# Cached keys and values loaded in 512 KB blocks, three at a time, and B's attention in another order of work

## The reference

```python
def diff_attn_sample(q, k_new, v_new, k_past, v_past, lam):
    s = concatenate([einsum('bqhcd,bkhcd->bhcqk', q, k_past), einsum('bqhcd,bkhcd->bhcqk', q, k_new)], -1) * scale
    p = softmax(s)
    pd = p[:, :, 0] - lam * p[:, :, 1]
    return einsum('bhqk,bkhe->bqhe', pd[..., :p_len], v_past) + einsum(..., pd[..., p_len:], v_new)

def fox_sample(q, k_new, v_new, logf_new, k_past, v_past, logf_past):
    f_cum = cumsum(concatenate([logf_past, logf_new], 1), 1)
    s_past = einsum('bqhd,bkhd->bhqk', q, k_past) * scale + f_q[..., None] - f_past
    s_new = einsum('bqhd,bkhd->bhqk', q, k_new) * scale + f_q[..., None] - f_new     # causal
    p = softmax(concatenate([s_past, s_new], -1))
    return einsum('bhqk,bkhd->bqhd', p[..., :p_len], v_past) + einsum(..., p[..., p_len:], v_new)
```

## Time and profile before

| | us |
|---|---|
| median of 3 runs | 2518.02 (2517.57 to 2519.05) |
| the profiled execution | 2516.69 |
| its span, first to last instruction | 2514.2 |
| PE busy | 2463.0 |
| VectorE busy | 1687.4 |
| ScalarE busy | 1134.2 |

### The profile page before, as it was taken

How to read it: one execution, slowest core, us unless ns; L and a number is a source line. 1 busy time by engine, 2 the same in 40 slices (tenths; PEclk the granted TensorE clock), 3 DMA queues, 4 the chain that set the end, 5 groups by cost and what they waited for, 6 DMA issues and landing times.

```text
span 2514.2 us, 46820 instructions
## 1 busy us (share of the span) xinstructions
PE 2463.0 (98%) x18869; PEld 2333.4 (93%) x18869; DVE 1687.4 (67%) x2936; ACT 1134.2 (45%) x2261; POOL 192.3 (8%) x136
## 2 busy tenths in 40 slices
PE   8999999999898999999999999999998899999998
PEld 8999999888678999999988999999986599999998
DVE  7777676322797886758625786858626677868585
ACT  6443444101785543435413553525327755535254
POOL 0000000543000000000044000000120000000000
PEclk9999999999999999999999999999999999999999
DMA  4323232233762232323233332222359631322222
GB/s 129 91 72 95 70 99 61 82 117 102 293 236 76 63 105 62 99 76 91 62 80 125 106 109 81 74 87 72 114 192 314 226 109 47 111 79 74 86 72 80
DMA packets 267136, 271.45 MB, mean 108 GB/s; under 512 B 13785, under 2 KB 224034, under 8 KB 266930
## 3 DMA queue, kind: packets, MB, share of 16 engines
q1 hardware_dynamic: 261184, 253.45, 32.4%
q10 hardware_dynamic: 5746, 15.12, 1.7%
HBM read 255.02 MB, written 13.51 MB: 107 GB/s over the span
## 4 chain that ended last, share of the span: by engine, by line
PE 90%; DVE 5%; ACT 2%; issue 2%; DMA 1%; DVEq 0%; POOL 0%; ACTq 0%
PE PS L769 40%; PE PS L875 24%; PE PS L956 10%; PE PS L719 7%; PE PS L707 2%; PE PS L1014 1%; PE PS L702 1%; PE PS L1157 1%; PE PS L1115 1%; DMA R<-in_cache_b_k_dram 1%; PE PS L1076 1%; PE PS L1087 1%; DVE x_area L2050 0%; DVE R L2005 0%; ACT R L1646 0%
## 5 line engine op out<-in xcount | busy, mean ns | idle before, releaser
L769 PE MATMUL PS<-x_area,w_area 128*128 128x320 f32 x3096 | 482.1, 309 | 0.0
L769 PEld LDWEIGHTS PS<-x_area,w_area 128*128 128x128 f32 x3096 | 461.0, 188 | 0.2 <-DVE w_area L1991 0.2
L875 PE MATMUL PS<-r_area,w_area 128*128 128x320 f32 x2568 | 393.3, 309 | 0.0
L875 PEld LDWEIGHTS PS<-r_area,w_area 128*128 128x128 f32 x2568 | 380.7, 188 | 0.8 <-DVE r_area L2183 0.8
L1435 ACT ACTIVATE w_area<-R 128x512 fp32r<-128x512 f32 x341 | 212.7, 628 | 200.4 <-PE PS L769 133.0
L1982 DVE TENSOR_TENSOR w_area<-R,w_area 128x768 fp32r<-128x768 f32 (+2 forms) x143 | 132.4, 926 | 218.5 <-ACT w_area L1420 216.9
L1991 DVE TENSOR_TENSOR w_area<-R,w_area 128x512 fp32r<-128x512 f32 x341 | 234.4, 688 | 47.6 <-ACT w_area L1435 41.8
L1420 ACT ACTIVATE w_area<-R 128x768 fp32r<-128x768 f32 (+2 forms) x143 | 117.0, 818 | 308.2 <-PE PS L875 281.2
L875 PE MATMUL PS<-v_area,w_area 128*128 128x320 f32 x1620 | 253.5, 309 | 0.0
L956 PE MATMUL PS<-w_area,xn_hi 128*128 128x512 f32 x800 | 251.0, 395 | 0.0
L875 PEld LDWEIGHTS PS<-v_area,w_area 128*128 128x128 f32 x1620 | 241.5, 188 | 0.3 <-DVE v_area L2183 0.3
(11 more groups left out here) (297 smaller groups left out, 3566.6 us busy)
## 6 DMA issues: line engine op xcount, KB each, us to landing
R<-in_w_ffn_up_dram SPq DMA_DIRECT2D x88, 512.0 KB, 3.9
R<-in_w_ffn_gate_dram SPq DMA_DIRECT2D x84, 512.0 KB, 3.9
R<-in_w_ffn_down_dram SPq DMA_DIRECT2D x96, 384.0 KB, 3.2
vreg<-in_cache_a_v_dram SPq DMA_DIRECT2D x8, 2048.0 KB, 9.0
vreg<-in_cache_b_v_dram SPq DMA_DIRECT2D x8, 2048.0 KB, 9.5
R<-in_cache_a_k_dram SPq DMA_DIRECT2D x14, 1024.0 KB, 7.2
R<-in_cache_b_k_dram SPq DMA_DIRECT2D x14, 1024.0 KB, 9.8
R<-in_w_qkv_a_dram SPq DMA_DIRECT2D x24, 512.0 KB, 3.8
```

Source lines behind the costliest of these rows:

```text
L769: last = pe.matmul(PS[:, bank, 0:HT], a[:, k, :], b[:, k, :], start=(start and k == 0 and a is hi and b is x_hi), stop=(k == 3 and a is lo ...
L875: last = pe.matmul(out[:, h, :], a[slot][:, w], x[:, h * HT:(h + 1) * HT], start=(k == 0 and a is w_hi and x is hi), stop=(k == n - 1 and ...
```

## The change

1. Keys are loaded in four blocks of 128 rows x all 1024 columns (512 KB, rows of 4 KB) instead of two halves of 4 heads. `Knat[:, k, :]` is row block `k`. Blocks 0 and 2 share one semaphore, 1 and 3 the other; SP waits for the landing of block `k - 2` before it asks for block `k`.
2. Values are loaded in four blocks in the same manner.
3. `key_pair(b, j)` becomes `key_turn(b, j)`: it turns row block `j` of all 8 heads (again 16 half turns) and needs that block alone. Its reads go to `kTc[:, :, j * 128 ...]`.
4. SP asks for each key block as soon as it is turned, and splits the values around the last key block. At the start of A it waits for the last projection tile, then asks for all of values 0, then keys 1, then the first tile of the output weights; before, keys 1 were first.
5. B's order of steps changes on PE, ScalarE and VectorE. A's order stays, but for the new key step.

```diff
-        Knat = R1[:, 0:4096].rearrange("p (s k c) -> p s k c", s=2, k=PB)
+        Knat = R1[:, 0:4096].rearrange("p (k c) -> p k c", k=PB)
...
+        def keys_landed(b, k):
+            return 16 + (b - 1) * 32 + (k // 2 + 1) * 16
+        def values_landed(x, b, k):
+            return ("AB".index(x) * DB + b) * 32 + (k // 2 + 1) * 16
...
+                def keys(b, k):
+                    at = sem(f"k_in{x}{k % 2}")
+                    sp.wait_ge(at, keys_landed(b, k) - 16)
+                    sp.dma_start(Knat[:, k, :], key_rows[x][b, k * P:(k + 1) * P, :]).then_inc(at, 16)
+                def values(b, blocks):
+                    for k in blocks:
+                        at = sem(f"v_in{k % 2}")
+                        if k >= 2:
+                            sp.wait_ge(at, values_landed(x, b, k) - 16)
+                        sp.dma_start(Vc[:, k, :], vc[b][k * P:(k + 1) * P, :]).then_inc(at, 16)
...
-                sp.wait_ge(sem("kt_ready" + x), 4)
-                keys(1, 0)
                 if x == "A":
+                    sp.wait_ge(w_used, BASE["oa"])
+                    values(0, range(PB))
+                    sp.wait_ge(sem("kt_readyA"), 8)
+                    for k in range(PB):
+                        keys(1, k)
                     tile(BASE["oa"], SLOT["oa"], *cols(w_o_a[0], SLOT["oa"], 0))
-                    sp.wait_ge(sem("kt_readyA"), 8)
-                    keys(1, 1)
-                    sp.wait_ge(w_used, BASE["oa"])
-                else:
+                else:
+                    sp.wait_ge(sem("kt_readyB"), 8)
+                    keys(1, 0)
+                    keys(1, 1)
                     sp.wait_ge(w_used, BASE["ob"] - 1)
                     rows(0)
                     forget(0, 0)
+                    keys(1, 2)
+                    keys(1, 3)
...
-                    if i + 2 < DB:
-                        sp.wait_ge(sem("kt_ready" + x), (i + 1) * 8 + 4)
-                        keys(i + 2, 0)
-                    if f_scr is not None and i + 2 < PAIR:
-                        sp.wait_ge(sem("nb_ready" + x), i * 4 + 4)
-                        rows(i + 2)
+                    for k in range(3):
+                        if more:
+                            sp.wait_ge(sem("kt_ready" + x), (i + 1) * 8 + 2 * k + 2)
+                            keys(i + 2, k)
+                        if k == 1 and f_scr is not None and i + 2 < PAIR:
+                            sp.wait_ge(sem("nb_ready" + x), i * 4 + 4)
+                            rows(i + 2)
                     sp.wait_ge(sem("pv_ready" + x), i * 2 + 2)
-                    values(i + 1)
-                    if i + 2 < DB:
+                    values(i + 1, (0, 1))
+                    if more:
                         sp.wait_ge(sem("kt_ready" + x), (i + 1) * 8 + 8)
-                        keys(i + 2, 1)
+                        keys(i + 2, 3)
+                    values(i + 1, (2, 3))
...
 # PE, key step
-                    for h in range(2):
-                        at = (2 * j + h) % 4 * P
-                        for k in range(PB):
-                            for r in range(2):
-                                to = (4 * h + k) * 64
-                                last = half_flip(PS[:, 3 + 4 * r, to:to + 64], Knat[:, j // 2, k, at:at + P], r)
+                    for h in range(PAIR):
+                        for r in range(2):
+                            last = half_flip(PS[:, 3 + 4 * r, 64 * h:64 * h + 64], Knat[:, j, h * P:(h + 1) * P], r)
...
 # PE, a round of B
                         stream_scores(i)
+                        stream_flips(i - 1)
                         output_columns(i - 1)
-                        stream_flips(i - 1)
+                        key_turn(i + 1, 0)
                         prompt_scores(x, i, (3,))
                         turn(i, 0)
-                        key_pair(i + 1, 0)
                         stream_turn(i)
                         turn(i, 1)
-                        key_pair(i + 1, 1)
+                        key_turn(i + 1, 1)
+                        prompt_scores(x, i + 1, (0, 1))
+                        stream_turn_new(i)
                         turn(i, 2)
-                        stream_turn_new(i)
-                        key_pair(i + 1, 2)
-                        prompt_scores(x, i + 1, (0, 1))
+                        key_turn(i + 1, 2)
                         stream_values(i)
-                        key_pair(i + 1, 3)
+                        key_turn(i + 1, 3)
+                        turn(i, 3)
                         prompt_scores(x, i + 1, (2,))
-                        turn(i, 3)
...
 # ScalarE, a round of B
                         stream_exps(i)
+                        key_turn(i + 1, 0)
                         turned(i, 0)
-                        key_pair(i + 1, 0)
                         differences(i)
+                        key_turn(i + 1, 1)
                         turned(i, 1)
-                        key_pair(i + 1, 1)
+                        exps(i, 3)
+                        key_turn(i + 1, 2)
                         turned(i, 2)
-                        exps(i, 3)
-                        key_pair(i + 1, 2)
                         exps(i + 1, 0)
+                        key_turn(i + 1, 3)
                         exps(i + 1, 1)
-                        key_pair(i + 1, 3)
...
 # VectorE, a round of B
                         stream_peaks(i)
+                        stream_output(i - 1)
                         output_columns(i - 1)
-                        stream_output(i - 1)
                         combine(i, 1)
+                        peaks(i, (3,))
+                        stream_norms(i)
+                        differences(i)
                         combine(i, 2)
-                        peaks(i, (3,))
-                        differences(i)
-                        stream_norms(i)
                         new_differences(i)
```

More of the change, by code:

```diff
@@ L586, in load_attention @@
                     rows(1)
-                    sp.wait_ge(sem("kt_readyB"), 8)
-                    keys(1, 1)
                     sp.wait_ge(w_used, BASE["ob"])
-                values(0)
+                    values(0, range(PB))
                 for i in range(DB - 1):
+                    more = i + 2 < DB
                     if f_scr is not None:
@@ L994, in first_keys @@
             def first_keys(x, h, bank):
-                pe.wait_ge(sem(f"k_in{x}{h // 4}"), 16)
+                for s in range(2):
+                    pe.wait_ge(sem(f"k_in{x}{s}"), 16)
                 if h >= 2:
@@ L999, in first_keys @@
                 for k in range(PB):
-                    last = flip(PS[:, bank, k * P:(k + 1) * P], Knat[:, h // 4, k, (h % 4) * P:(h % 4 + 1) * P])
+                    last = flip(PS[:, bank, k * P:(k + 1) * P], Knat[:, k, h * P:(h + 1) * P])
                 last.then_inc(sem("kt_ready" + x), 1)
@@ L1028, in attend, with key_turn @@
                 pT, qbd = turned_probs[x], queries[x]
-                reads, first_pair_reads = (5, 2) if x == "A" else (4, 1)
-                def key_pair(b, j):
+                reads, first_reads = (5, 2) if x == "A" else (4, 1)
+                def key_turn(b, j):
                     if b == DB:
                         return
-                    if j % 2 == 0:
-                        pe.wait_ge(sem(f"k_in{x}{j // 2}"), b * 16 + 16)
+                    pe.wait_ge(sem(f"k_in{x}{j % 2}"), keys_landed(b, j))
                     if j == 0:
@@ L1104, in stream_scores @@
                     if b >= 1:
-                        pe.wait_ge(sem("pairs_read" + x), reads * b)
+                        pe.wait_ge(sem("keys_read" + x), reads * b)
                     else:
@@ L1147, in stream_values @@
                 def stream_values(b):
-                    pe.wait_ge(sem("v_in" + x), b * 16 + 16)
+                    for k in (2, 3):
+                        pe.wait_ge(sem(f"v_in{k % 2}"), values_landed(x, b, k))
                     for r in range(2):
@@ L1667, in key_pair @@
                     for r in range(1 if x == "A" and j == 0 else 2):
-                        last = act.activation(kTc[:, 2 * j:2 * j + 2, :].rearrange("p h (k r q) -> p r (h k) q", k=PB, r=2)[:, r],
-                                              PS[:, 3 + 4 * r, :].rearrange("p (n q) -> p n q", q=64), ACT.Copy)
-                    last.then_inc(sem("pairs_read" + x), 1)
+                        at = j * P + 64 * r
+                        last = act.activation(kTc[:, :, at:at + 64], PS[:, 3 + 4 * r, :].rearrange("p (h q) -> p h q", q=64), ACT.Copy)
+                    last.then_inc(sem("keys_read" + x), 1)
                 def stream_exps(b):
@@ L2466, in attend @@
                         stream_output(i - 1)
[L2467 removed]
+                        first_uppers(i + 1)
                         differences(i)
```

32 lines of the change are left out of this document (13 added, 19 removed).

## The result

The changed kernel took 2533.15 us (median of 5, 2530.18 to 2534.27) against 2517.57 beside it: 1.0060 of the time before, 95% interval 1.0045 to 1.0075. It is slower by 15.6 us. The forecast was 2507 in a range of 2500 to 2519: the time lies outside the range and on the other side of no change. The profiled execution is one of the five, with a span of 2531.2 us (2514.2 before), so 17.0 us have to be found.

The account below looks back on a forecast made before the run. TensorE, busy 98%, was taken as the bound, so only its waits and lower clock could be won. Loads in B -6.0, in A -3.2, A's opening +3.0, B's order -5.0 gave -11.2 us from 2518.02: 2507 us, range 2500 to 2519.

Parts of the forecast that it names:

- What bounds the kernel: Whole kernel: TensorE is busy 98% of the span, so only time in which it waits or runs at the lower clock can be won.
- "issue" stalls: PE gaps amid turns in A's and B's attention, no semaphore waited for; read as instruction loads behind bulk transfers, 1.29 to 2.05 us.
- Costed at nothing: SP's waits for landings: SP's queue in B: new waits for landings were taken to delay nothing needed in time, so 0 us in the sum.
- that cover: B: last values block placed 3 us into the next round, forget and prompt rows behind it; forget rows' release at about 4.
- the second rival: B's loads: fewer bytes in flight starve B, +3.3 us in each of seven rounds, about 2540 us; chance 0.09.
- Loads in blocks, B: B's attention: smaller blocks end code stalls and key waits in three disturbed rounds, -6.0 us, bounds -6.0 and 0.
- Loads in blocks, A: A's attention, rounds 1 and 2: both fall to the undisturbed 15.65 us, -3.2 us, bounds that and 0.
- A's opening: A's first round: keys 1 queue behind values 0 and ScalarE's store, first key block at 642.5; +3.0 us, bounds -1.6 and +6.
- Rival 4: A's opening costs +9 instead of +3, last key blocks and stream 1's values being late; 2513 us, chance 0.10.
- B's order: B's rounds: new order on three engines leaves 0.56 us of gaps for 1.18, -0.62 a round, -5 in eight; bounds 0 and -9.4.
- Rival 3: B's order pays nothing, the wait moves to turn 2 in full, stalls are gone; 2512 us, chance 0.15.
- The chances: Whole kernel: 0.64 for faster by over 0.2%, 0.09 for slower by over 0.2%, 0.27 for no change; main case 0.50.

## Why the prediction was wrong, point by point

*What bounds the kernel* held. PE has the same 18869 instructions and is busy for 2465.3 us (2463.0 before), so all 17 us are waits and clock. That the "issue" stalls are late code held too, and that they hang on the bulk bytes: with a quarter of these none is left of 0.55 us or more. That the code packet stands in line behind them is not shown, and the evidence I read it from, some 10 us without a code packet, is found in a clean round too; the stall shows in the packet coming after PE has stopped.

*Costed at nothing: SP's waits for landings.* This is the step that failed. I looked for who is queued behind the last values block, found forget and prompt rows, and placed that block 3 us into the next round. It was issued about 9 us in, and landed 15.6 us in (1955.15 to 1970.77). I had counted only the last link. The chain is: key block 0 lands (9.1 us), key block 2, values 0 and 1, values 0 lands (4.6 us), values 2 and 3, last landing (6.7 us). Each link was taken at the 3.9 us of loaded weights or less. The price of the values' links, by taking them out, is (1.0060 - 1.0022) x 2517.6 = 9.6 us, where the sum had nothing; the keys' link, the longest, added nothing measurable. "If that cover fails, the second rival is what happens" was right: the rival's mechanism (fewer bytes in flight starve B) is the main cause: B's rounds 0 to 5 moved 278 GB/s, and 311 without landing waits. A's new loading, 8.1 us by its own removal, is nearly as large. The rival's price was too high, 2540 for 2533, and its chance of 0.09 too low: the sum of landing latencies was to be had from SP's order in the diff and was not walked, while PE's order was.

*Loads in blocks, B: -6.0.* It came out worse than its other bound of 0: 4.39 and 1.85 us of code stalls instead of 1.29 and 1.88, and 7.3 us of waits for values. I had argued that at most three blocks stand ahead of a code packet. But the limit of two in flight is one for keys and one for values, and forget rows, prompt rows and new keys are outside both: behind each wait SP lets them go in one burst. Without any landing waits the stalls are 2.49 and 2.12. So block size did not help the code; the bytes decide.

*Loads in blocks, A: -3.2.* 1.3 of it came. Round 2 took 15.82 (17.00 before), round 1 17.36 (17.51) with a stall of 1.73 us. Against this the later rounds had a floor 0.16 higher (15.81), 0.14 of it right in front of `stream_values` and gone where PE waits for one semaphore there.

*A's opening: +3.0.* It was +8.2, beyond its upper bound of 6. PE had the first key block at 645.77, 642.5 was taken and 638 to 645 was the range, since I let it queue behind 2.1 MB of values on the DMA engines, but SP asked for it only at 636.17, after two landings of values. And the lower clock was left out of that term. The granted clock was 0.74 in that round; PE had idled for 11.31 us, and the first key turn behind that took 1.12 us where the one of the earlier trace rows took 0.71; PE's busy time in the round is 13.98 against 13.17. Undoing the order, the chain or both (27.07, 25.54, 26.05 us) does not mend it; moving the store does half (22.27) and only shifts it. Rival 4 had the size (+9) by luck and not the mechanism: the wait came at the first key block, none came at the last ones, and A's second round, over 17 us (17.36), had a code stall and no wait for values.

*B's order: -0.62 a round, -5.* The walk found the right place and was near in size. Its largest wait, before turn 2, is there in each round. By the walk it shows as a gap of 0.46 (0.65 less 0.19), and it is 0.62 in the later rounds (0.70 and 0.87 in the first two). The clean round, 16.37 with a wait for values of 0.71, is 15.66 without it, and 15.59 in other kernels; the walk gave 15.9. What failed here is to multiply it by eight: a shorter round needs its bytes sooner. At 5.3 MB, 16.52 us ask for 321 GB/s and 15.6 us for 340. With the order alone the loads of the earlier trace rows were late twice, and the measured gain was 0.0003 with an interval on both sides of 1. Rival 3 too had no gain from the order, but by the wait at turn 2; here the time went to waits for keys.

*The chances.* I gave 0.09 to slower. Three of four terms were bounded at zero from above without a row that excludes a loss; the landing waits stood in the list of free edits though the trace of before has no such wait at all.

## What to carry to other kernels

A wait for a landing on the queue's engine is a serial chain through everything issued behind it: walk that engine's program as PE's is walked, with the landing time under load, and ask when the last transfer of the chain is issued, not who is late behind it. Where time is spent waiting for bytes, a shorter compute round gives nothing unless the bytes come sooner as well, so test order and loads separately. And smaller blocks free their space later if they cut across the order in which it is used, as row blocks against heads did here.

## What the runs showed of the hardware

- A 512 KB load landed after 3.8 us where only weights are loaded, and after 5.2 and 7.2 us (values and keys of B) where two or more sources share SP's queue; single ones took 9.1 us.
- Blocks of 512 KB are no limit by themselves. Without landing waits A's round 0 moved 379 GB/s, as much as the 380 with blocks of 1 and 2 MB, the 2.6 MB store being in both:

```profile
630.06:655.60 25.54, 13.21 (x253) 9.71 (x250) 11.21 (x30) 11.88 (x36) 0.58 (x2) 0.80 1.03 379
```

  The Trainium skill (DMA: Bandwidth & Descriptors, Bandwidth) asks for 1 MiB or more per DMA for 75% of peak. This row does not agree for loads several deep: how many are in flight mattered here, the size did not. No run shows a load alone.
- A code stall costs more than itself. The `stream_scores` behind the 4.39 us one took 3.38 us, against 1.92 in the undisturbed round; the clock granted over the two rounds was 0.92. It was 0.50 from PE's restart to these scores, the lower of its two levels (1.2 GHz), 0.56 over the scores, and 1.00 over the scores at 1938.78. PE's timeline of the changed kernel:

```profile
1921.01 3.38 PE L1132 MATMUL PS<-R,vreg 128*32 128x512 f32 x16
```
```profile
1938.78 1.92 PE L1132 MATMUL PS<-R,vreg 128*32 128x512 f32 x16
```

- PE went on 2.2 to 2.9 us after a code packet in all 55 code stalls, over the kernel before, the changed one and its variants. Packets 10 us apart are no sign of a stall (1921.9 and 1932.1 in the clean round of before); a packet that comes after PE has stopped is. How the packets are held up stays open, since no view shows when one was asked for. The Trainium skill (DMA: Bandwidth & Descriptors, Queues, rings and completion order) says that each DMA engine turns round-robin between the queue rows with work, packet by packet. A packet of SP's took 0.12 us (971 in 8 us on 16 engines, 92.3% busy), so by that rule a code packet that has been asked for waits for little more than that, and the rule alone doesn't explain a stall of 4.39 us. For the store on ScalarE's queue the trace agrees in kind: the key wait fell from 11.31 to 6.70 us when the store was moved.
